# Three reorderings in a fused four-layer plus two-layer forward pass on one Trainium2 core: output pieces, one eviction and two high-part copies moved

## The chip, the cores and the metric

The kernel runs on one core of a Trainium2 chip. The engines of the core work at the same time, each through its own list of instructions in order: TensorE (PE) multiplies matrices into the PSUM banks, VectorE (DVE) and ScalarE (ACT) work on tiles in SBUF and PSUM, GpSimd (POOL) works on tiles in SBUF, and SyncE (SP) issues the loads. They wait for each other on semaphores. The metric is the device time of one execution in microseconds. Lower is better.

## The reference, cut to what matters

Six layers on a sequence of 256 tokens with 1024 channels: convolution, sparse attention, latent attention (MLA), convolution, pooling, stick-breaking attention. The change touches the two softmax attentions and the pooling layer.

```python
def dsa_mixer(...):      # 16 heads of 64; keys chosen by an indexer
    logits = where(chosen, q @ k.T * scale, -inf)
    o = softmax(logits) @ v
    return (o * silu(z)) @ w_out

def mla_mixer(...):      # 16 heads of 96; q and kv from low-rank latents
    logits = where(chunk_visible, q @ k.T * scale, -inf)
    o = softmax(logits) @ v
    return (o * silu(z)) @ w_out

def pooling_mixer(u, w_in, w_group, scale, w_out):
    xb, z = split(u @ w_in, 2)
    xg = xb.reshape(B, S, 4, 512)
    pooled = [causal_pool_minus_self(xg[:, :, g], w) for g, w in enumerate((2, 4, 8, 16))]
    mixed = einsum('bsgi,gio->bsgo', pooled, w_group)
    return (mixed * scale * silu(z)) @ w_out
```

## The kernel before

**Precision.** Every float32 factor of a large matmul is split into a high part and a low part, and a product is three matmuls: high by high, high by low, low by high (`three`). For weights, ACT makes the high part (`whi`, L483 for halves of a unit and L491 for quarters) and DVE subtracts it from the loaded tile to get the low part (`wlo`, L930 and L951).

**Units.** The weights come as a row of units, each a load into one of two `raw` slots, a split, and a run of matmuls. Units are counted by `unit_done`; the load of a unit waits until the slot's earlier unit has its low part (`lo_ready`). A unit of 512 columns is 96 matmuls; `B0`, `C0`, `P0` are the numbers of the first units of the sparse, the latent and the pooling layer.

**The softmax stages** (`paired_heads` on PE, `softmax_heads` on ACT and DVE) run over the 16 heads in steps j = 0 to 9, two heads a step. In step j PE issues the scores of heads 2j and 2j+1, the product with the values for the pair j-2, filler 2j, the transposes of the probabilities of heads 2j-2 and 2j-1 (L2133), and filler 2j+1. DVE does in step j: two minima (L1268, L1272; PE waits for them as `logits`), the gate `ytmp` of pair j-2 (L1253), weight quarters (L951) and two divisions (L1277, L1279). ACT does the exponentials (L705, L707), the copies of the transposes (L720) and the high parts of the weight quarters (L491). POOL splits the gated output into `yh` and `yl` (L1693, L1583).

**Fillers** are matmuls that depend on little and are placed between the dependent ones. First come the pieces of the units for v and z, in parts of 24 matmuls. The last z unit (B0+9, C0+7, called z1) sits in banks 2 and 3 of `acc` and is evicted by `take` (L1038). Then come the output pieces: `attention_out(u, y0, k, half)` is 12 matmuls (k row of the first output unit, half of the columns). Those of half 0 write the `acc` banks that z1 occupied, so the first of them waits for `z_raw`, the semaphore of that eviction. Those of half 1 write the `aux` banks of the scores, so they wait for all 16 `logits`. `out_filler` (L2044) says at which filler number each piece stands: for half 0 the four numbers `at`, for half 1 fillers 15 and 16. The other two pieces of half 1 and the whole second unit follow the loop (`attention_last_out`).

**The pooling stage** runs the list of units x0, z0, x1, mix0, z1, x2, mix1, z2, x3, mix2, z3, mix3, where x and z are columns of the input projection for a group and mix is the group's own matrix. PE starts unit i once unit i-2 has been evicted. For a group, DVE evicts x into `pad` (L1464), POOL forms the pooled sum in several passes (L1747), scales it (L1752) and subtracts (L1753), ACT writes the high part `ph` (L842, `pooled_high`), and POOL the low part `pl` (L1755). The mix unit waits for `pl_ready`. While it handles unit i, ACT also splits the weights of unit i+2. DVE in a z unit takes the low part of unit i+2, then the low part of the earlier y (L1454), then evicts z (L1473).

Of the kernel before, what the change touches and what calls it, by code (L numbers as in the profile page):

```python
# [46 lines left out]
A0, B0, C0, A1, P0, S0, END = 0, 10, 22, 32, 42, 58, 74  # L47
# [51 lines left out]
def build(nc, a, out):  # L99

    ctx = ExitStack()
    with ctx:
# [217 lines left out]
        def quarters(u, halves):  # L320

            return {step: tuple((u, 2 * half + n) for n in range(2)) for half, step in enumerate(halves)}

        SPARSE_SPLITS = {**quarters(B0 + 9, (0, 1)), **quarters(B0 + 10, (2, 3)), **quarters(B0 + 11, (5, 8))}
        MLA_SPLITS = {0: ((C0 + 7, 2), (C0 + 7, 3)), **quarters(C0 + 8, (2, 3)), **quarters(C0 + 9, (5, 8))}
        SPARSE_TANH = {0: (24,), 1: (26,), 4: (28,), 5: (30,)}
        MLA_TANH = {1: (40,), 2: (42,), 4: (44,), 5: (46,)}
        FILLERS = (("v", 1), ("z", 1), ("z", 2), ("v", 2), ("z", 3), ("v", 3))
# [119 lines left out]
        def _(act):  # L448
# [348 lines left out]
            for c in range(4):  # L797
# [3 lines left out]
                h, g = 4 * (c % 2), c // 2  # L801
# [38 lines left out]
            def pooled_high(g):  # L840
                act.wait_ge(sem("pooled"), g + 1)
                A(ph[:, :, :], pad[2][:, :, 16:16 + T], ACT.Copy).then_inc(sem("ph_ready"), 1)  # L842

            for i, (kind, g) in enumerate(POOL_UNITS):
                if kind == "x":
                    split(P0 + i + 2)
                elif kind == "z":
                    split(P0 + i + 2)
                    if g == 0:
                        pooled_high(0)  # L850
                    act.wait_ge(sem("z_raw"), 4 + g + 1)
                    A(arena[:, 39:43, :], arena[:, 39:43, :], ACT.Silu).then_inc(sem("z_ready"), 1)
                else:
                    y_count[0] += 1
                    dst = (yh if g < 2 else y2h)[:, 4 * (g % 2):4 * (g % 2) + 4, :]
                    split(P0 + i + 2, (0, 1) if g == 2 else (0,))
                    if g == 2:
                        pooled_high(3)
                    y_high(y_count[0], dst, arena[:, 39:43, :])
                    if g != 2:  # L860
                        split(P0 + i + 2, (1,))
                    if g < 2:
                        pooled_high(g + 1)
            split(P0 + 14)
            split(P0 + 15)
            split(S0)
# [12 lines left out]
            for i in range(HEADS + 1):  # L879
                if i in FILLED:  # L880
                    kind, n = FILLERS[FILLED.index(i)]
# [18 lines left out]
                if i - 1 in FILLED and FILLERS[FILLED.index(i - 1)][0] == "z":  # L900
                    n = FILLERS[FILLED.index(i - 1)][1]
# [22 lines left out]
        def _(dve):  # L924
# [105 lines left out]
            def take(u, t, name, scale=None, s=None, space=acc):  # L1030

                dve.wait_ge(unit_done, u + 1)
                for c in range(2):
                    src, dst = two(space[:, 2 * (u % 2 if s is None else s) + c, :]), arena[:, t + 2 * c:t + 2 * c + 2, :]
                    if scale is None:
                        ins = TT(dst, src, rb, ALU.mult)
                    else:
                        ins = STT(dst, src, scale, rb, ALU.mult, ALU.mult)  # L1038
                ins.then_inc(sem(name), 1)
# [218 lines left out]
            def softmax_heads(layer, bias, z0):  # L1258
# [23 lines left out]
                for j in range(HEADS // 2 + 2):  # L1282
                    if j < HEADS // 2:
                        minima(2 * j)
                        minima(2 * j + 1)
                    for t in (SPARSE_TANH, MLA_TANH)[layer].get(j - 1, ()):
                        half_silu(t)
                    if j == 9:
                        for u, q in splits[8]:
                            split_quarter(u, q)  # L1290
                    if j >= 2:
                        t = j - 2
                        gate(t, z0, acc[:, 0, T * (t % 2):T * (t % 2) + T], h0 + 2 * t + 2, 4 * layer + t // 2 + 1)
                    for n in range(2):
                        if layer == 0 and j == 4 and n:
                            take(B0 + 9, 28, "z_raw", 0.5)
                        if j - 1 in splits and j < 9:
                            split_quarter(*splits[j - 1][n])
                        if j < HEADS // 2:
                            division(2 * j + n)  # L1300
                    if layer == 1 and j == 0:
                        q_factor(1)
                    if layer == 1 and j == 3:
                        take(C0 + 7, 44, "z_raw", 0.5)

            softmax_heads(0, pick, 24)
            split(C0)
# [62 lines left out]
            for c in range(4):  # L1370
# [16 lines left out]
                if c % 2:  # L1387
                    g = c // 2
# [6 lines left out]
            for c in range(4):  # L1395
# [3 lines left out]
                h, g = 4 * (c % 2), c // 2  # L1399
# [368 lines left out]
        def _(pe):  # L1768
# [274 lines left out]

            def out_filler(f, layer):  # L2044

                u, y0, at = (C0 + 8, 16, (9, 11, 12, 13)) if layer else (B0 + 10, 8, (10, 11, 12, 13))
                if f == at[0]:
                    taken("z_raw", 2 * layer + 2)
                if f in at:
                    attention_out(u, y0, at.index(f), 0)  # L2050
                if 15 <= f < 17:
                    if f == 15:
                        taken("logits", HEADS * layer + HEADS)
                    attention_out(u, y0, f - 15, 1)

            def attention_out(u, y0, k, half):

# [227 lines left out]
            for i in range(HEADS + 2):  # L2285
# [16 lines left out]
                if i < len(FILL):  # L2302
                    f, k0, kn = FILL[i]
# [86 lines left out]
```

## Time and profile before

| | us |
|---|---|
| median of 3 runs | 937.6 |
| lowest and highest | 936.26, 938.47 |
| profiled execution, its own time | 938.38 |
| its span, first to last instruction | 936.7 |
| PE busy, share of the span | 904.1, 97% |
| DVE busy | 648.0, 69% |
| ACT busy | 493.8, 53% |
| POOL busy | 313.6, 33% |
| mean granted TensorE clock | 0.993 of full speed |

PE is busy nearly all the time, so the time can only move where PE waits, or where its clock is granted at half speed. The softmax of the sparse layer lies at about 228 to 287 us of the span, that of the latent layer at about 360 to 415, and the pooling units at 543 to 664. A row of the timeline gives start, duration, engine, line, operation with output and inputs, how many are merged, and in brackets the idle time of the engine before it and what ended it.

### The profile page before, as it was taken

What the parts mean: (1) busy time and instruction counts of PE and PEld (TensorE: products, weight loads), DVE (VectorE), ACT (ScalarE), POOL (GpSimd) and SP (SyncE); (2) the same over time, 40 slices, a digit from 0 to 9 for tenths busy, and PEclk for the clock granted to TensorE, in tenths of its full rate; (3) what the DMA queues carried; (4) which work ended last, traced back from release to release, by engine and by line L of the source; (5) the groups of instructions that cost most, each with busy time, mean ns of one, the idle gap of its engine ahead of it and who ended that gap; (6) DMA issues with size and microseconds to landing.
All of it is one profiled execution on the core that took longest, in us unless ns stands there. A gap on an engine that the chain in (4) does not pass through costs nothing.

```text
span 936.7 us, 16801 instructions
## 1 busy us (share of the span) xinstructions
PE 904.1 (97%) x6761; PEld 850.3 (91%) x6761; DVE 648.0 (69%) x1023; ACT 493.8 (53%) x716; POOL 313.6 (33%) x259
## 2 busy tenths in 40 slices
PE   5999999999989999999999999999999999999996
PEld 5999997788879988779999999999999998989996
DVE  5687666889885789965776676687636645656642
ACT  5544445664765659755444454353535336586632
POOL 7543323373122342233343218775003000223310
PEclk9999999999999999999999999999999999999998
DMA  9796436344314443445695535354663652424411
GB/s 249 194 239 196 180 104 231 124 141 172 143 60 150 141 141 116 133 113 153 163 228 198 180 135 181 135 172 151 247 240 133 236 181 91 172 99 179 156 49 45
DMA packets 123585, 148.70 MB, mean 159 GB/s; under 512 B 9561, under 2 KB 79102, under 8 KB 123518
## 3 DMA queue, kind: packets, MB, share of 16 engines
q1 hardware_dynamic: 121472, 145.63, 48.0%
q10 hardware_dynamic: 1582, 1.12, 0.4%
q0 software_dynamic: 464, 1.02, 0.3%
q8 instruction: 47, 0.77, 0.3%
q14 instruction: 20, 0.16, 0.1%
HBM read 146.70 MB, written 1.05 MB: 158 GB/s over the span
## 4 chain that ended last, share of the span: by engine, by line
PE 62%; DVE 10%; ACT 4%; POOL 3%; issue 1%; ACTq 0%; POOLq 0%; DVEq 0%
PE acc L1770 44%; PE aux L1770 17%; DVE wlo L930 3%; POOL pad L1747 2%; DVE wlo L951 1%; DVE work L1268 1%; DVE work L1279 1%; POOL sqy L1684 1%; ACT work L707 1%; ACT work L705 1%; PE aux L2133 1%; POOL pad L1752 0%; ACT work L720 0%; ACT whi L491 0%; DVE arena L1038 0%
## 5 line engine op out<-in xcount | busy, mean ns | idle before, releaser
L930 DVE TENSOR_TENSOR wlo<-raw,whi 128x2048 fp32r<-128x2048 f32 (+5 forms) x114 | 270.4, 2393 | 90.7 <-ACT whi L483 88.7
L1770 PE MATMUL acc<-xh,whi 128*128 128x256 f32 x1128 | 322.4, 286 | 1.4 <-DVE wlo L930 0.8
L1770 PE MATMUL acc<-xl,whi 128*128 128x256 f32 x1128 | 319.6, 283 | 0.0
L1770 PE MATMUL acc<-xh,wlo 128*128 128x256 f32 x1128 | 319.5, 283 | 0.0
L483 ACT ACTIVATE whi<-raw 128x2048 fp32r<-128x2048 f32 (+5 forms) x115 | 197.8, 1745 | 89.1 <-PE acc L1770 48.3
L1770 PEld LDWEIGHTS acc<-xh,whi 128*128 128x128 f32 x1128 | 216.5, 192 | 3.5 <-issue 1.5
L1770 PEld LDWEIGHTS acc<-xl,whi 128*128 128x128 f32 x1128 | 216.6, 192 | 0.0
L1770 PEld LDWEIGHTS acc<-xh,wlo 128*128 128x128 f32 x1128 | 216.4, 192 | 0.0
L1693 POOL CAST yh<-ytmp 128x256 fp32r<-128x256 f32 x24 | 24.3, 1012 | 207.7 <-DVE ytmp L1532 119.1
L1770 PE MATMUL aux<-yh,whi 128*128 128x256 f32 x288 | 82.6, 287 | 2.0 <-DVE stat L1272 2.0
L1770 PE MATMUL acc<-whi,xh 128*128 128x512 f32 (+1 forms) x208 | 81.4, 391 | 1.6 <-DVE arena L1038 0.5
L1770 PE MATMUL aux<-yh,wlo 128*128 128x256 f32 x288 | 81.9, 284 | 0.0
L1770 PE MATMUL aux<-yl,whi 128*128 128x256 f32 x288 | 81.8, 284 | 0.0
L1770 PE MATMUL acc<-whi,xl 128*128 128x512 f32 (+1 forms) x208 | 78.8, 379 | 0.0
L1770 PE MATMUL acc<-wlo,xh 128*128 128x512 f32 (+1 forms) x208 | 78.8, 379 | 0.0
L951 DVE TENSOR_TENSOR wlo<-raw,whi 128x1024 fp32r<-128x1024 f32 x54 | 66.6, 1236 | 1.7 <-ACT whi L491 1.7
L1770 PEld LDWEIGHTS aux<-yh,whi 128*128 128x128 f32 x288 | 55.6, 193 | 3.3 <-DVE stat L1272 2.5
L1770 PEld LDWEIGHTS aux<-yh,wlo 128*128 128x128 f32 x288 | 55.6, 193 | 0.0
L1770 PEld LDWEIGHTS aux<-yl,whi 128*128 128x128 f32 x288 | 55.6, 193 | 0.0
L491 ACT ACTIVATE whi<-raw 128x1024 fp32r<-128x1024 f32 x52 | 53.2, 1047 | 0.0
L1770 PEld LDWEIGHTS acc<-whi,xh 128*128 128x128 f32 x208 | 39.1, 188 | 12.1 <-issue 4.1
L551 ACT ACTIVATE yh<-arena 128x256 f32 (+1 forms) x16 | 6.7, 418 | 82.2 <-DVE arena L1077 82.2
(344 smaller groups left out, 1726.4 us busy)
## 6 DMA issues: line engine op xcount, KB each, us to landing
raw<-in_a_w_in SPq DMA_DIRECT2D x52, 512.0 KB, 6.6
raw<-in_sb_w_in SPq DMA_DIRECT2D x48, 512.0 KB, 5.2
raw<-in_b_w_in SPq DMA_DIRECT2D x36, 512.0 KB, 5.3
raw<-in_pool_w_in SPq DMA_DIRECT2D x32, 512.0 KB, 5.6
raw<-in_a_w_out SPq DMA_DIRECT2D x16, 512.0 KB, 5.0
raw<-in_pool_w_out SPq DMA_DIRECT2D x16, 512.0 KB, 5.8
raw<-in_sb_w_out SPq DMA_DIRECT2D x16, 512.0 KB, 5.2
raw<-in_b_w_out SPq DMA_DIRECT2D x8, 512.0 KB, 5.0
```

The costliest lines, as they stand in the source:

```text
L483: A(whi[b][:, lo:hi], (raw_third if third else raw[b])[:, lo:hi], ACT.Copy).then_inc(hi_ready, 1)
L491: ins = A(whi[u % 2][:, c * q:c * q + c], raw[u % 2][:, c * q:c * q + c], ACT.Copy)
L705: A(L[:, 0:P], L[:, 0:P], ACT.Exp, bias=st[:, 0:1], scale=nf[:, i:i + 1], accum_out=st[:, 2:3])\
L707: A(L[:, P:W384], L[:, P:W384], ACT.Exp, bias=st[:, 1:2], scale=nf[:, HEADS + i:HEADS + i + 1], accum_out=st[:, 3:4]).then_inc(sem("exp_re ...
L930: TT(wlo[b][:, lo:hi], (raw_third if third else raw[b])[:, lo:hi], whi[b][:, lo:hi].bitcast(F32), ALU.subtract).then_inc(lo_ready, 1)
L951: ins = TT(wlo[u % 2][:, c], raw[u % 2][:, c], whi[u % 2][:, c].bitcast(F32), ALU.subtract)
L1268: ins = V.tensor_tensor_reduce(L[:, lo:hi], S[:, lo:hi], bias[:, lo:hi], -1.0, 3.0e38, ALU.add, ALU.min, st[:, n:n + 1])
L1279: ins = TS(L[:, lo:hi], L[:, lo:hi], st[:, 2 + n:3 + n], None, ALU.mult)
L1684: ins = TT(raw, raw, f.rearrange("p (h d) -> p h d", d=1).broadcast_to([P, 8, 64]), ALU.mult)
L1693: nc.gpsimd.tensor_copy(hi, ytmp[:, :]).then_inc(sem("yh_ready"), 1)
L1747: me.link(TT(pad[dst][:, :, lo:16 + T], pad[src][:, :, lo:16 + T], pad[src][:, :, lo - w:16 + T - w], ALU.add))
L1770: return nc.tensor.matmul(out_, lhsT, rhs, start=start, stop=stop, skip_group_check=True)
```

## The change

1. `MLA_SPLITS`: the second half of the latent layer's first output unit (C0+8) is split in step 4 of ACT and step 5 of DVE, not 3 and 4.
2. Latent softmax on DVE: z1 is evicted (`take`) in step 4 between the two divisions, as in the sparse layer, not at the end of step 3.
3. `out_filler`: the half 0 pieces stand at fillers 11, 12, 13, 15 (sparse, before 10, 11, 12, 13) and 9, 11, 13, 15 (latent, before 9, 11, 12, 13); the first two of half 1 stand at 16 and 17, before 15 and 16.
4. Pooling on ACT: the high parts of the pooled groups 1 and 2 are written in the following z unit, behind the split of the weights of mix1 and mix2, and no longer at the end of the mix unit ahead of it.

```diff
-        MLA_SPLITS = {0: ((C0 + 7, 2), (C0 + 7, 3)), **quarters(C0 + 8, (2, 3)), **quarters(C0 + 9, (5, 8))}
+        MLA_SPLITS = {0: ((C0 + 7, 2), (C0 + 7, 3)), **quarters(C0 + 8, (2, 4)), **quarters(C0 + 9, (5, 8))}
...
-                    if g == 0:
-                        pooled_high(0)
+                    if g < 3:
+                        pooled_high(g)
...
-                    if g < 2:
-                        pooled_high(g + 1)
...
-                        if layer == 0 and j == 4 and n:
-                            take(B0 + 9, 28, "z_raw", 0.5)
+                        if j == 4 and n:
+                            take(C0 + 7 if layer else B0 + 9, 44 if layer else 28, "z_raw", 0.5)
...
-                    if layer == 1 and j == 3:
-                        take(C0 + 7, 44, "z_raw", 0.5)
...
-                u, y0, at = (C0 + 8, 16, (9, 11, 12, 13)) if layer else (B0 + 10, 8, (10, 11, 12, 13))
+                u, y0, at = (C0 + 8, 16, (9, 11, 13, 15)) if layer else (B0 + 10, 8, (11, 12, 13, 15))
...
-                if 15 <= f < 17:
-                    if f == 15:
+                if 16 <= f < 18:
+                    if f == 16:
                         taken("logits", HEADS * layer + HEADS)
-                    attention_out(u, y0, f - 15, 1)
+                    attention_out(u, y0, f - 16, 1)
```

The orders below are the instructions of one engine in a row. The line numbers of the changed kernel are 2 to 4 lower from the pooling code on.

DVE in the latent softmax, around step 4, before (L1038 is the eviction of z1, L1253 the gate of pair 2, L951 a weight quarter, L1277 and L1279 a division):

```order
L1038 SCALAR_TENSOR_TENSOR arena<-acc,r 128x512 x2
L1268 ISA work,stat<-aux,mask 128x128
...
L1253 TENSOR_TENSOR ytmp<-acc,arena 128x256
L951 TENSOR_TENSOR wlo_53<-raw_49,whi_51 128x1024
L1277 RECIPROCAL stat<-stat 128x2
L1279 TENSOR_SCALAR work<-work,stat 128x128
L1279 TENSOR_SCALAR work<-work,stat 128x256
L951 TENSOR_TENSOR wlo_53<-raw_49,whi_51 128x1024
L1277 RECIPROCAL stat<-stat 128x2
```

The same place after:

```order
L1266 ISA work,stat<-aux,mask 128x128
...
L1251 TENSOR_TENSOR ytmp<-acc,arena 128x256
L1275 RECIPROCAL stat<-stat 128x2
L1277 TENSOR_SCALAR work<-work,stat 128x128
L1277 TENSOR_SCALAR work<-work,stat 128x256
L1036 SCALAR_TENSOR_TENSOR arena<-acc,r 128x512 x2
L1275 RECIPROCAL stat<-stat 128x2
```

The eviction went from ahead of the minima of heads 8 and 9 to behind the division of head 8, and the two weight quarters left step 4.

PE in the sparse softmax, steps 5 and 6, before (L2133 transposes of two heads, `yh,whi` the first matmul of an output piece, `work,vB` the product with the values):

```order
L1770 MATMUL acc<-work,vB 64x256 x2
L1770 MATMUL acc<-work,vB 64x128 x2
L1770 MATMUL acc<-yh,whi_51 128x256
...
L1770 MATMUL acc<-yh,wlo_53 128x256
L2133 MATMUL aux<-cst,work 128x128 x6
L1770 MATMUL acc<-yh,whi_51 128x256
```

The same place after:

```order
L1766 MATMUL acc<-work,vB 64x256 x2
L1766 MATMUL acc<-work,vB 64x128 x2
L2129 MATMUL aux<-cst,work 128x128 x6
L1766 MATMUL acc<-yh,whi_51 128x256
...
L1766 MATMUL acc<-yh,wlo_53 128x256
L1766 MATMUL aux<-arena 128x128 x2
```

The output piece that stood ahead of the transposes of heads 8 and 9 is gone from there, and every piece is one place later.

ACT in the pooling stage, from the end of mix0 to x2, before (L842 the high part of a pooled group, the pair `128x1024 x2` the weights of mix1, L852 the silu of z1):

```order
L483 ACTIVATE whi_52<-raw_50 128x2048
L842 ACTIVATE ph<-pad_70 128x1024
L483 ACTIVATE whi_51<-raw_49 128x1024 x2
L852 ACTIVATE arena<-arena 128x1024
L483 ACTIVATE whi_52<-raw_50 128x2048 x2
```

The same place after:

```order
L483 ACTIVATE whi_52<-raw_50 128x2048
L483 ACTIVATE whi_51<-raw_49 128x1024 x2
L842 ACTIVATE ph<-pad_70 128x1024
L852 ACTIVATE arena<-arena 128x1024
L483 ACTIVATE whi_52<-raw_50 128x2048 x2
```

The split of mix1's weights and the high part of group 1 changed places.

## Rows read from the trace of the kernel before

**Rows 1.** The page: the chain that ended last, share of the span by engine.

```profile
PE 62%; DVE 10%; ACT 4%; POOL 3%; issue 1%; ACTq 0%; POOLq 0%; DVEq 0%
```

**Rows 2.** Waits of PE, whole span: waiter, releaser, total us, times, longest.

```profile
PE acc L1770 <- ACT work L720: 3.8, 7, 0.6
...
PE acc L1770 <- DVE arena L1473: 2.0, 1, 2.0
PE aux L1770 <- DVE stat L1272: 2.0, 2, 1.0
```

**Rows 3.** Timeline of PE, pooling: first matmul of mix1 and of z2.

```profile
610.32 0.58 PE L1770 MATMUL acc<-ph,whi 128*128 128x256 f32 x1 [2.04 <-DVE arena L1473]
...
617.62 0.28 PE L1770 MATMUL acc<-xh,whi 128*128 128x256 f32 x1
```

**Rows 4.** Stretches: length, busy of PE, PEld, DVE, ACT, POOL, granted clock, DMA.

```profile
406.00:408.00 2.00, 2.00 (x10) 1.47 (x11) 0.72 (x3) 2.00 (x6) 0.53 (x1) 0.50 0.00 0
...
610.30:612.00 1.70, 1.69 (x8) 1.69 (x9) 1.16 (x2) 1.70 (x2) 0.40 (x1) 0.50 1.13 387
```

**Rows 5.** The chain that ended last: a run of matmuls at full clock.

```profile
664.09 46.08 PE aux L1770 x384
```

**Rows 6.** Timeline of ACT, pooling, around the split of mix1's weights.

```profile
602.04 1.06 ACT L842 ACTIVATE ph<-pad 128x1024 fp32r<-128x1024 f32 x1 [8.73 <-POOL pad L1753]
603.00 1.99 ACT L483 ACTIVATE whi<-raw 128x1024 fp32r<-128x1024 f32 x2
```

**Rows 7.** Timeline of DVE, the same stretch.

```profile
593.35 3.90 DVE L930 TENSOR_TENSOR wlo<-raw,whi 128x2048 fp32r<-128x2048 f32 x1 [0.52 <-ACT whi L483]
604.15 3.66 DVE L930 TENSOR_TENSOR wlo<-raw,whi 128x1024 fp32r<-128x1024 f32 x2 [6.90 <-ACT whi L483]
607.73 1.21 DVE L1454 TENSOR_TENSOR yl<-arena,yh 128x1024 fp32r<-128x1024 f32 x1
608.97 1.29 DVE L1473 TENSOR_TENSOR arena<-acc,r 128x512 f32<-128x512 f32 x2
```

**Rows 8.** Timeline of POOL, the same stretch.

```profile
595.18 4.34 POOL L1752 TENSOR_TENSOR pad<-pad,count 128x1024 f32<-128x1024 f32 x1
599.60 2.41 POOL L1753 TENSOR_TENSOR pad<-pad,pad 128x1024 f32<-128x1024 f32 x1
603.17 2.41 POOL L1755 TENSOR_TENSOR pl<-pad,ph 128x1024 fp32r<-128x1024 f32 x1 [1.17 <-ACT ph L842]
```

**Rows 9.** Timeline of DVE, latent softmax, step 4.

```profile
384.48 1.28 DVE L1038 SCALAR_TENSOR_TENSOR arena<-acc,r 128x512 f32<-128x512 f32 x2
...
387.60 1.22 DVE L951 TENSOR_TENSOR wlo<-raw,whi 128x1024 fp32r<-128x1024 f32 x1
...
388.92 1.10 DVE L1279 TENSOR_SCALAR work<-work,stat 128x128 f32<-128x128 f32 x2
...
391.27 0.55 DVE L1279 TENSOR_SCALAR work<-work,stat 128x128 f32<-128x128 f32 x2
391.73 0.28 DVE L1268 CUSTOM_DVE_ANT_0 work<-aux,mask 128x128 f32<-128x128 f32 x1
```

**Rows 10.** Timeline of PE, latent: transposes 6 and 7, first output piece, scores 10 and 11.

```profile
384.83 0.88 PE L2133 MATMUL aux<-cst,work 128*128 128x128 f32 x6
385.82 0.39 PE L1770 MATMUL acc<-yh,whi 128*128 128x256 f32 x1
...
387.36 1.58 PE L1770 MATMUL aux<-arena 96*128 96x128 f32 x8
```

**Rows 11.** Timeline of PE, sparse softmax, end of the stage.

```profile
277.46 0.39 PE L1770 MATMUL aux<-yh,whi 128*128 128x256 f32 x1 [1.00 <-DVE stat L1272]
...
279.68 0.87 PE L1770 MATMUL acc<-work,vB 128*64 128x256 f32 x8 [0.54 <-ACT work L720]
...
282.01 0.82 PE L2133 MATMUL aux<-cst,work 128*128 128x128 f32 x6
283.46 0.87 PE L1770 MATMUL acc<-work,vB 128*64 128x256 f32 x8 [0.63 <-ACT work L720]
```

## The prediction

> **What bounds the kernel now.** I read the chain that ended last first: PE holds most of it [rows 1], and PE is busy 97% of the span, so a reordering pays only where PE waits or where its clock is granted at half speed. The waits of PE come next [rows 2]. The reader is to see two kinds: one wait of 2.04 us for the eviction of a z unit (L1473), and short ones for the copies of the transposes and the last minima in the two softmax stages. The first sits in the pooling stage: mix1 starts at 610.32 after 2.04 us without work [rows 3]. The granted clock of the stretches around it is the third view. From 610.3 on it stands at 0.50, which is 1.2 GHz of the two levels 1.2 and 2.4, and the same happens at 406 to 408 us, in the tail of the latent softmax [rows 4]. The price of this in pooling: mix1 is 48 matmuls. At full clock a matmul takes 46.08/384 = 0.12 us [rows 5], so mix1 should take 5.76 us, and it takes 617.62 - 610.32 = 7.30 [rows 3]. So the wait cost 2.04 and the lower clock behind it 1.54, together 3.6 us.
>
> Why PE waits there: mix1 reuses the banks of z1, which DVE evicts at 608.97 to 610.26 [rows 7]. DVE was late because it takes the low part of mix1's weights first (604.15 to 607.81), for which ACT gave the high part only at 603.00 [rows 6, 7]. And ACT stood 8.73 us in front of the high part of the pooled group, waiting for POOL, with the split queued behind [rows 6].
>
> **Pooling, the two high parts moved: a gain.** With the split first, ACT waits only for the end of unit z1. Unit x2 (96 matmuls, 11.5 us) ends at 608.28, so z1 ends at 596.8. The split of the two halves takes 1.99 [rows 6], so they are written by 598.8, if the weights have landed by 596.8; their slot was free from the split of x1's unit on, two units before. DVE is free at 597.25 [rows 7]. Its two halves cost about 1.1 each and now fall beside POOL's L1752 and L1753. POOL's L1752 took 4.34 us while DVE's L930 ran to 597.25, L1753 took 2.41 with DVE idle, and both are 1024 columns [rows 7, 8]. So I let them take turns: POOL to 599.5, DVE half to 600.6, POOL's L1753 to 603.1, DVE half to 604.2. The high part `ph` then comes at 603.1 to 604.2. The low part of y (1.2) and `pl` (2.41) [rows 7, 8] take turns again: `pl` is ready at about 607.8, where before it was 605.6. The eviction of z1 (1.29) ends at about 606.8. Unit x2 ends at 608.28, so all is ready by some 0.5 us and the wait of 2.04 goes, and with it what made the clock fall. The gain is 2.04 + 1.54 = 3.6. The split of z2's weights also comes earlier by the same amount and meets POOL's first pass, so I take 3.5. Bounds: 3.6, and 1.5 if 0.5 us of wait are left and the clock falls all the same. Group 2 has no wait of PE before it and `ph` is later by some 2 us with more than 5 to spare, so I cost it at nothing; its cover is unit x3.
>
> The Trainium skill (SBUF — State Buffer, SBUF: two separate sides) says that VectorE with two SBUF inputs and GpSimd take a shared port pair as an exclusive lock for the whole instruction. The 4.34 beside 2.41 agrees. By that rule, if DVE got both its halves in ahead of L1753, `pl` would come at 608.5, 0.2 us too late, and the gain would be 3.4; were there no lock, it would come at about 605.6 and the gain would be 3.6. It leaves the sum where it is.
>
> **Sparse softmax, pieces one place on: a small loss.** Up to the product with the values at 279.68, which waits for ACT's copies [rows 11], the pace is set by DVE and ACT, which the change leaves alone here: the piece no longer in front of the transposes of heads 8 and 9 leaves PE idle, for division 9 is late. From 279.68 on PE's own work counts. Before, it does product, piece, transposes (282.01), waits 0.63, product (283.46), then two pieces. After, one more piece stands behind the transposes: it starts at about 282.6, ends at 284.1, and hides the wait of 0.63. The last product moves from 283.46 to 284.1: 0.7 us lost. The wait of 1.00 for the last minima (277.46) is filled with a piece, but that only brings PE earlier to the same 279.68. Bounds: 0, if PE is held elsewhere anyway, and 2.2 if the idle time up to 279.68 now joins into one stretch of 2 us and the clock falls as it did after 2.04.
>
> **Latent softmax: a loss.** This part has three terms.
> *The eviction behind division 8.* In the kernel before, DVE evicts z1 at 384.48 to 385.76 and PE's first output piece starts at 385.82, right on it [rows 9, 10]. After, DVE starts the minima of heads 8 and 9 at 384.5 (the scores are ready by then, since PE is past them and past the product behind them at 384.83 [rows 10]), then the gate, then division 8. From eviction to the first quarter, two minima and the gate take 387.60 - 385.68 = 1.9, so the gate ends at 386.4. Division 8 costs 0.1 to 0.2 for the reciprocal (388.92 less the end of L951 at 388.82, and its own wait for the exponentials) plus 1.10 while POOL splits the gated pair [rows 9]: 387.8. Then the eviction, 1.28: 389.1. The piece at filler 9 has not moved and needs it, so PE stands from 385.7 to 389.1. Behind it in PE's queue are the scores of heads 10 and 11. The piece is 1.54 (385.82 to 387.36) and the scores 1.5 [rows 10], so they are ready at 392.2. DVE has finished division 9 (0.75) at 389.9 and has nothing else, as the quarters left this step: it idles 2.3 us. From 384.5 to the end of the stage DVE was busy nearly without a gap, and its work up to the last minima is only reordered, the two quarters (1.22 each) coming in step 5. So its idle time goes straight into the end: 2.3, call it 2.4 with worse collisions. Filling PE's later waits gives nothing back, since DVE and ACT set the pace.
> *The clock.* PE has 3.4 us without work there, more than the 2.04 after which the clock fell in pooling [rows 3, 4]. I expect half speed for the piece and perhaps the scores: 12 matmuls cost 12 x 0.12 = 1.4 more at most, less where the fall comes early and is spent idle; I take 1.1. The fall at 406 now costs about 0.8; I let it recur, as the tail keeps waits of the same size.
> *The tail,* as in the sparse stage: one piece more behind transposes 14 and 15, 0.7.
> Sum 4.2; bounds 2.3 (clock kept, and the present fall gone too) and 5.7 (a second fall in the tail, at the 1.54 of pooling).
>
> **Sum.** 0.7 + 4.2 - 3.5 = +1.4 on the profiled execution of 938.38, whose span is 936.7. That execution is 0.8 above the median of 937.6, and I carry the difference over: 939.0. In per cent it is +0.15. What a measurement of this kernel can tell from no change is about 0.2%, 1.9 us.
>
> **Rivals.**
> *Slower, the gain is smaller:* the clock fall in pooling is not in most executions of the kernel before, or comes at another place after. Then pooling gives 2.0 and the sum is 0.7 + 4.2 - 2.0 = +2.9: 940.5. For it: a gap of 1.00 at 276.5 brought no fall [rows 11], so 2.04 may lie near the border. Against it: in this execution the clock was down as soon as work resumed. It decides the sign of the verdict from a pooling gain under 3.0 on. Chance 0.33.
> *Slower, a new fall in a tail:* 1.5 more, 940.5 to 942. For it: waits join, as the piece at 277.46 moves up. Against: the gaps of 1.00 and 0.54 there brought none. Chance 0.07.
> *Faster:* the latent wait is not on the path. If the eviction ended by 386.8, scores 10 and 11 would meet DVE right when it ends division 9, and latent would cost only its tail: 0.7 + 0.7 - 3.5 = -2.1, 935.5. It would take exponentials and division 8 done 2.3 us earlier than the rows allow. With the clock kept in the latent stage and its present fall gone, the sum is 0.7 + 2.3 - 3.5 = -0.5, which is still no change. Chance 0.05.
> *The change does not do what it says:* the orders show that it does; only `pl` too late is left, 0.5 us, inside the range.
>
> **Numbers.** The forecast holds 0.55: no change within 0.2%. Slower holds 0.33 + 0.07 = 0.40, faster 0.05. The low end takes 0.7 + 2.3 - 3.5 = -0.5, down to 937.0; the high end takes the first slower rival with 1 us of a second fall: 941.4.
>
> **What the profile after would show.** Pooling: no wait of PE for the z eviction, mix1 in 5.8 us, clock 1.00 there. Latent: PE waiting some 3.4 us for the eviction (L1036), DVE idle over 2 us before the minima of head 10, clock 0.50 in the next piece. Sparse: PE idle some 1.9 us before the product that stood at 279.68, no wait at the last one. A latent wait under 1 us, or a wait for `pl` in pooling, would prove me wrong.

## The result, and the profile after

The changed kernel takes 938.78 us (median, 936.47 to 940.63), beside 937.61 us of the kernel before on the same chip. The ratio is 1.0014, interval 1.0007 to 1.0020: 1.2 us slower, clear of zero and inside the 0.2% called no change. Forecast were 939.0 and +1.4. The profiled execution has its own time of 939.35 and a span of 937.7 us, 1.0 above the span of before.

The waits of PE over the whole span (waiter, releaser, total us, times, longest). The line numbers of the changed kernel are 4 lower than before on PE and 2 lower in the softmax code of DVE:

```profile
PE acc L1766 <- ACT work L720: 4.0, 5, 1.8
PE aux L2129 <- DVE work L1277: 3.9, 5, 1.2
PE acc L1766 <- DVE arena L1036: 3.4, 2, 2.9
```

Against [rows 2] the wait for the eviction of a z unit in pooling (L1473, 2.0 us) is gone, and one of 2.9 us for the eviction of z1 in the latent softmax (L1036) has come. The copies (L720) are waited for fewer times and once for longer. The waits for the last minima of the two softmax stages (L1272, 2.0 us) are gone too, filled with pieces.

**Pooling.** PE, the first matmul of mix1 and of z2, the rows that answer to [rows 3]:

```profile
612.61 0.28 PE L1766 MATMUL acc<-ph,whi 128*128 128x256 f32 x1
...
618.53 0.36 PE L1766 MATMUL acc<-xh,whi 128*128 128x256 f32 x1
```

No wait stands in brackets, and mix1 takes 618.53 - 612.61 = 5.92 us where it took 7.30. ACT, DVE and POOL in the same stretch, to be read beside [rows 6 to 8]:

```profile
601.35 2.01 ACT L483 ACTIVATE whi<-raw 128x1024 fp32r<-128x1024 f32 x2 [3.53 <-PE acc L1766]
607.40 1.06 ACT L842 ACTIVATE ph<-pad 128x1024 fp32r<-128x1024 f32 x1 [4.04 <-POOL pad L1749]
```

```profile
597.86 3.89 DVE L928 TENSOR_TENSOR wlo<-raw,whi 128x2048 fp32r<-128x2048 f32 x1 [0.54 <-ACT whi L483]
602.51 5.94 DVE L928 TENSOR_TENSOR wlo<-raw,whi 128x1024 fp32r<-128x1024 f32 x2 [0.77 <-ACT whi L483]
608.38 1.21 DVE L1450 TENSOR_TENSOR yl<-arena,yh 128x1024 fp32r<-128x1024 f32 x1
609.62 1.29 DVE L1469 TENSOR_TENSOR arena<-acc,r 128x512 f32<-128x512 f32 x2
```

```profile
599.67 4.36 POOL L1748 TENSOR_TENSOR pad<-pad,count 128x1024 f32<-128x1024 f32 x1
604.11 3.26 POOL L1749 TENSOR_TENSOR pad<-pad,pad 128x1024 f32<-128x1024 f32 x1
608.54 3.33 POOL L1751 TENSOR_TENSOR pl<-pad,ph 128x1024 fp32r<-128x1024 f32 x1 [1.18 <-ACT ph L842]
```

The split of mix1's weights is released by PE's z1 and no longer stands behind `ph`. The two low parts on DVE (5.94 us) and POOL's L1749 (3.26 where it took 2.41) stretch each other. Short stretches of DVE's rows of L928 show where the first half ends (length, busy time, instructions in it, clock, DMA):

```profile
605.10:605.15 0.05, 0.05 (x2) 1.00 0.94 369
605.15:605.20 0.05, 0.05 (x1) 1.00 1.05 410
```

Two instructions overlap up to 605.15 and one is left behind it, so the first half ends there. The eviction ends at 610.91 and `pl` at 611.87; unit x2 ends at 612.61, so what PE needs is there 0.74 us early. The stage is 4.5 us later than in the trace of before when it starts (its first matmul of `xh` by `whi` at 559.03, at 554.53 before) and 0.99 later when it ends (the run of 384 matmuls at 665.08, at 664.09 before): -3.5.

**Latent softmax.** DVE, step 4 and the start of step 5, beside [rows 9]; then PE, beside [rows 10]:

```profile
388.62 0.55 DVE L1277 TENSOR_SCALAR work<-work,stat 128x128 f32<-128x128 f32 x2
389.08 1.28 DVE L1036 SCALAR_TENSOR_TENSOR arena<-acc,r 128x512 f32<-128x512 f32 x2
...
390.48 0.55 DVE L1277 TENSOR_SCALAR work<-work,stat 128x128 f32<-128x128 f32 x2
394.57 0.29 DVE L1266 CUSTOM_DVE_ANT_0 work<-aux,mask 128x128 f32<-128x128 f32 x1 [3.55 <-PE aux L1766]
```

```profile
386.69 0.88 PE L2129 MATMUL aux<-cst,work 128*128 128x128 f32 x6
390.42 0.50 PE L1766 MATMUL acc<-yh,whi 128*128 128x256 f32 x1 [2.85 <-DVE arena L1036]
...
393.07 1.90 PE L1766 MATMUL aux<-arena 96*128 96x128 f32 x8
```

PE stands 2.85 us for the eviction. The piece then takes 393.07 - 390.42 = 2.65 us, where it took 1.54. The scores behind it take 1.90 for 1.58, and DVE idles 3.55 us for them. The granted clock of these stretches, with one later and one in pooling (columns as in [rows 4]):

```profile
390.00:393.00 3.00, 2.58 (x12) 2.58 (x13) 0.99 (x4) 2.61 (x4) 0.00 (x0) 0.59 0.00 0
393.00:396.00 3.00, 3.00 (x21) 2.31 (x20) 1.39 (x9) 0.55 (x3) 0.00 (x0) 0.84 0.03 5
...
408.00:411.00 3.00, 3.00 (x14) 3.00 (x15) 2.52 (x15) 2.31 (x9) 1.03 (x2) 0.50 0.56 138
...
612.00:615.00 3.00, 3.00 (x27) 3.00 (x26) 1.47 (x3) 2.14 (x3) 0.76 (x1) 1.00 0.99 363
```

The fall in pooling is gone, one at 390 has come, and the one in the tail of the latent softmax is there as before, some 2 us later.

**Sparse softmax.** PE at the end of the stage, beside [rows 11] (two products with the values, and between them the transposes of heads 14 and 15):

```profile
280.81 0.87 PE L1766 MATMUL acc<-work,vB 128*64 128x256 f32 x8 [1.79 <-ACT work L720]
283.15 0.82 PE L2129 MATMUL aux<-cst,work 128*128 128x128 f32 x6
285.33 0.87 PE L1766 MATMUL acc<-work,vB 128*64 128x256 f32 x8
```

The idle time is joined into one wait of 1.79 us, and the last product has none. It comes 1.87 us later than the one of 283.46, of which 1.14 is an offset that the trace has before the stage.

In the two traces the parts are therefore: sparse +0.73, latent +2.65 (below), pooling -3.5, and the offset of 1.1 that lies ahead of all three.

### The profile page after: what moved, and what is told of

It reads as the page before. It is cut to its first block, busy times and chain, and to the rows that moved or that the text cites. A ratio compares the mean times of both kernels' runs of the same rounds, so it can differ in the third digit from the quotient of the medians.

```text
span 937.7 us, 16801 instructions
## 1 busy us (share of the span) xinstructions
PE 904.1 (96%) x6761; PEld 851.5 (91%) x6761; DVE 653.5 (70%) x1023; ACT 494.1 (53%) x716; POOL 314.6 (34%) x259
## 4 chain that ended last, share of the span: by engine, by line
PE 64%; DVE 10%; ACT 3%; POOL 1%; issue 1%; ACTq 0%; POOLq 0%; DVEq 0%
PE acc L1766 46%; PE aux L1766 17%; DVE wlo L928 2%; DVE wlo L949 1%; DVE work L1277 1%; DVE work L1266 1%; POOL sqy L1680 1%; ACT work L707 1%; ACT work L705 1%; PE aux L2129 0%; ACT whi L491 0%; DVE arena L1036 0%; DVE sqy L1126 0%; DVE hf L1136 0%; ACT arena L745 0%
## 5 line engine op out<-in xcount | busy, mean ns | idle before, releaser
L928 DVE TENSOR_TENSOR wlo<-raw,whi 128x2048 fp32r<-128x2048 f32 (+5 forms) x114 | 273.6, 2421 | 81.9 <-ACT whi L483 80.0
```

Of the source, the lines that this page charges most:

```text
L928: TT(wlo[b][:, lo:hi], (raw_third if third else raw[b])[:, lo:hi], whi[b][:, lo:hi].bitcast(F32), ALU.subtract).then_inc(lo_ready, 1)
```

## The experiments

**The three parts alone.** Each kernel below is the kernel before with one part of the change.

`pool_only`, the pooling part:

```diff
-                    if g == 0:
-                        pooled_high(0)
+                    if g < 3:
+                        pooled_high(g)
...
-                    if g < 2:
-                        pooled_high(g + 1)
```

> Only the pooling part: the high parts of pooled groups 1 and 2 behind the split of the mix weights; both softmaxes as in the kernel before. Theory A (the wait of 2.04 us and the fall of the clock behind it both go): 3.5 us faster, about 934.1. Theory B (the fall of the clock is not there in most executions of the kernel before): only 2.0 us faster, about 935.6. In the profile both expect no wait of PE for the z eviction.

Measured: 934.51 us beside 937.41, ratio 0.9965 (0.9952 to 0.9978), -2.9 us (-3.3 by the ratio). Span 932.8.

`sparse_only`, the sparse output pieces:

```diff
-(B0 + 10, 8, (10, 11, 12, 13))
+(B0 + 10, 8, (11, 12, 13, 15))
...
-                if 15 <= f < 17:
+                late = 15 if layer else 16
+                if late <= f < late + 2:
```

> Only the output pieces of the sparse softmax one place on (11, 12, 13, 15 and 16, 17). Theory A (one more piece of 1.5 us behind the last copies, hiding a wait of 0.63): 0.7 us slower, about 938.3, first matmul after the last product 0.7 us later against the scores of heads 8 and 9. Rival (the joined idle time lets the clock fall): 1.5 to 2.2 us slower, with granted clock 0.50 behind the idle 1.8 us.

Measured: 937.28 us beside 937.41, ratio 1.0000 (0.9991 to 1.0008). In its trace the same stretch of the stage, from the scores at 256.60 to the last product at 284.61, is 28.01 us, 0.73 more than before and the same as in the whole change. Its times lie in two groups, six at 936.0 to 936.7 with a mean clock of 0.997 or 0.998, and six at 937.9 to 939.2 with 0.995 or 0.996. The 0.7 us is in the rows; in the time it is not shown.

`latent_only`, the split of the weights, the eviction and the pieces of the latent softmax:

```diff
-**quarters(C0 + 8, (2, 3))
+**quarters(C0 + 8, (2, 4))
...
-                        if layer == 0 and j == 4 and n:
+                        if j == 4 and n:
...
-(C0 + 8, 16, (9, 11, 12, 13))
+(C0 + 8, 16, (9, 11, 13, 15))
...
+                late = 16 if layer else 15
```

> Only the latent softmax part: eviction of z1 in step 4, second half of the first output unit split one step later, pieces at 9, 11, 13, 15 and 16, 17. Theory A: PE waits 2.9 us for the eviction and works at half clock behind it; 3.5 to 4.2 us slower in the median, about 941.4. Theory B (the pooling gain was 2.0, so the latent loss is what is left of the sum of 1.2): 2.5 us slower, about 940.1.

Measured: 941.59 us beside 937.41, ratio 1.0047 (1.0034 to 1.0059), +4.2 us. The parts add up: -2.9 + 0 + 4.2 = +1.3, and the whole is +1.2. The forecast was -3.5 + 0.7 + 4.2.

**Which row of the pooling part gives the gain.** `pool_g1` moves only the high part of group 1; that of group 2 stays where it was.

```diff
-                    if g == 0:
-                        pooled_high(0)
+                    if g < 2:
+                        pooled_high(g)
...
-                    if g < 2:
+                    if g == 1:
                         pooled_high(g + 1)
```

> The pooling part for group 1 alone; the high part of group 2 stays at the end of mix1. Theory A (only mix1 was waited for): the whole gain of the pooling part, 3.0 us, about 934.5. Rival (group 2 brings part of it): 935.5 or more.

Measured: 933.60 us beside 937.18, ratio 0.9964 (0.9950 to 0.9978). The gain is there with group 1 alone, and group 2 is worth nothing that shows, as its move was costed.

**Wait or clock in pooling.** `pool_warm` is the kernel before with 14 extra matmuls into a free bank ahead of mix1. The wait is there, filled with work.

```diff
+                if i == 6:
+                    for _ in range(14):
+                        mm(aux[:, 3, 0:T], xh[:, 0, 0:P], xh[:, 0, :], True)
```

> The kernel before with 14 extra matmuls (1.7 us, into a PSUM bank that nobody reads) on PE ahead of the wait for the z1 eviction in pooling; nothing else changes and the wait still ends at the same moment. Theory A (the lower clock behind the wait is a cost of its own, 1.5 us): mix1 takes 5.8 us at clock 1.00 and the kernel is 1.0 to 1.5 us faster, about 936.2, with the wait shrunk to some 0.4. Rival (the fall of the clock is not there in most executions): no change, 937.4.

PE ahead of mix1, and a stretch behind it:

```profile
608.29 1.84 PE L1770 MATMUL aux<-xh 128*128 128x256 f32 x14
610.49 0.39 PE L1770 MATMUL acc<-ph,whi 128*128 128x256 f32 x1 [0.36 <-DVE arena L1473]
```

```profile
612.00:614.00 2.00, 2.00 (x19) 2.00 (x18) 0.64 (x1) 2.00 (x2) 1.92 (x2) 1.00 1.01 376
```

Measured: 936.71 us beside 937.18, ratio 0.9996 (0.9987 to 1.0005). The clock stays at 1.00 behind mix1's start, and mix1 still starts where it did, so the wait of 2.04 is the part that the extra matmuls can't give back. The span falls by 1.2 us, and the median by 0.5 with an interval that holds zero. In the trace mix1 takes 616.34 - 610.49 = 5.85 us, 1.45 less than the 7.30 of before. So the fall costs about 1.5 us in an execution that has it, and the median, with an interval of -1.2 to +0.5 us, has less of it.

How often does the fall stand there? Seven traces are of kernels with the pooling part as before, and each has the wait, 2.04 to 2.08 us. In six of them (before, `sparse_only`, `latent_only`, `evict_only`, `latent_no_evict`, `lat_pieces`) mix1 takes 7.30 to 7.35 us. In `lat_quarters`, behind a wait of 2.06, it takes 5.86 at full clock.

**What of the latent part costs.** `evict_only` moves only the eviction of z1 behind division 8; the quarters and the pieces stay.

```diff
-                        if layer == 0 and j == 4 and n:
-                            take(B0 + 9, 28, "z_raw", 0.5)
+                        if j == 4 and n:
+                            take(C0 + 7 if layer else B0 + 9, 44 if layer else 28, "z_raw", 0.5)
...
-                    if layer == 1 and j == 3:
-                        take(C0 + 7, 44, "z_raw", 0.5)
```

> The kernel before with one edit: the latent z1 evicted in step 4 between the divisions; pieces and weight quarters as before. Theory A (PE stands at the first piece until the eviction, and the scores of heads 10 and 11 behind it come too late for DVE): the eviction now also has a weight quarter ahead of it and ends at about 390.3, but DVE has another quarter to do meanwhile, so it idles 1 to 2 us before the minima of head 10; 1.0 to 2.5 us slower, about 939.2. Rival (the eviction's place costs nothing and the moved pieces or quarters make the latent loss): no change, 937.4.

Its waits between 377 and 416 us:

```profile
DVE work L1268 <- PE aux L1768: 4.5, 3, 2.9
PE acc L1768 <- DVE arena L1038: 4.4, 1, 4.4
```

Measured: 940.48 us beside 937.18, ratio 1.0033 (1.0021 to 1.0044), +3.3. With both quarters still in step 4, PE waits 4.4 us instead of 2.9, and DVE's longest wait for the scores is 2.9.

`latent_no_evict` is `latent_only` with the eviction left at the end of step 3.

> The latent part without its eviction: quarters one step later and pieces at 9, 11, 13, 15 and 16, 17, z1 evicted at the end of step 3 as before. Theory A: the loss of 4.2 us that the latent part alone showed is gone; what is left is its tail, 0.7 us in the rows and nothing in the median, as the sparse part alone: 937.4 to 938.1. Rival (the quarters in step 5 lengthen DVE's path): still 2 us or more slower, over 939.4.

Measured: 939.26 us beside 937.18, ratio 1.0025 (1.0015 to 1.0036), +2.1. There is no long wait for the eviction, and still it is slower. Two kernels take it apart. `lat_quarters` has the first line of the diff of `latent_only` alone:

> The kernel before with one line of the latent part alone: the second half of C0+8 is split in step 4 of ACT and step 5 of DVE. The eviction of z1 and all output pieces stand where they stood. Run to take apart the 2.1 us (939.26 against 937.18) that the latent part without the moved eviction cost. Theory: the ACT splits stand ahead of the tanh that DVE's L1245 waits for (0.9 us there, 0.5 before), and the DVE splits ahead of two later divisions, so most of it is here: 938.2 to 939.2. Rival: it is the pieces, and this kernel is within 0.4 us of the one before.

`lat_pieces` has its pieces alone:

> The kernel before with the places of the latent output pieces alone: half 0 at fillers 9, 11, 13, 15, half 1 from filler 16. The weight quarters and the eviction of z1 stand where they stood. If the two parts add up to the 2.1 us measured for both together, this one gives what the other leaves: by the theory (the quarters cost it) 937.2 to 938.0; by the rival (one more piece of 12 matmuls stands behind the loop's last transposes, and DVE waits for the scores behind a piece) 938.5 to 939.5.

Measured: `lat_quarters` 937.64 us beside 937.41, ratio 1.0008 (1.0000 to 1.0017); `lat_pieces` 938.59 us, ratio 1.0016 (1.0007 to 1.0026). The theory that the quarters cost most of it falls: it is +0.2 for them and +1.2 for the pieces. Together that is 1.4 of the 2.1 by the medians, and 0.0024 of 0.0025 by the ratios. The rows of the table below say +0.57 for the quarters and +0.74 for the pieces, and +1.31, their sum, for both.

**The eviction's wait taken out of the whole change.** `at11` is the changed kernel with one number different, so that the first piece stands one step behind the eviction:

```diff
-(C0 + 8, 16, (9, 11, 13, 15))
+(C0 + 8, 16, (11, 12, 13, 15))
```

> The whole change, but with the latent output pieces at fillers 11, 12, 13, 15, so that the first one no longer stands between the eviction and the scores of heads 10 and 11. Theory A (the loss of the latent stage is the scores held up behind the piece that waits for z1): DVE has no idle time before the minima of head 10, the latent stage costs only its tail of 0.7, and the kernel is 0.7 + 0.7 - 3.5 = 2.1 us faster than before, about 935.5. Rival (the eviction itself, or the two weight quarters moved to step 5, is the cost): no better than the whole change, about 938.8.

Measured: 935.90 us beside 937.41, ratio 0.9990 (0.9981 to 0.9999), 2.9 below the changed kernel (2.2 by the ratios). Its trace has no stretch under full clock until PE's work is over.

`mended` is `at11` with the sparse pieces where they stood in the kernel before.

> The changed kernel with the sparse output pieces back where they stood and the latent pieces of half 0 at fillers 11, 12, 13, 15, so that PE does not come to them before the eviction of z1 is done. The pooling part is in full. Measured so far against the kernel before: the pooling part alone -2.9 us, the whole change with these latent pieces -1.3 us (935.9). Theory: the remaining 1.6 us between the two are the sparse pieces (0.7 us later in the rows) and the latent pieces at the end of the loop, and the moved eviction itself costs nothing: 934.5 to 935.2. Rival: the moved eviction and its divisions behind it cost about 1.5 us even with the first piece out of the way: 935.7 to 936.5. If it comes out under 934.0, the later eviction is a gain once the piece no longer waits for it.

DVE in steps 4 and 5 (the row of L1266 has no bracket), and PE's scores of heads 10 and 11:

```profile
387.01 1.28 DVE L1036 SCALAR_TENSOR_TENSOR arena<-acc,r 128x512 f32<-128x512 f32 x2
...
388.39 0.55 DVE L1277 TENSOR_SCALAR work<-work,stat 128x128 f32<-128x128 f32 x2
388.86 0.28 DVE L1266 CUSTOM_DVE_ANT_0 work<-aux,mask 128x128 f32<-128x128 f32 x1
```

```profile
385.95 1.58 PE L1766 MATMUL aux<-arena 96*128 96x128 f32 x8 [0.46 <-DVE stat L1270]
388.18 0.87 PE L1766 MATMUL acc<-work,vC 128*64 128x256 f32 x8 [0.64 <-ACT work L720]
```

Measured: 934.34 us beside 937.62, ratio 0.9971 (0.9959 to 0.9982). The eviction stands as late as in the changed kernel, but the scores of heads 10 and 11 end at 387.5, before the eviction does, and DVE goes from division 9 straight into the minima. The late eviction costs nothing once no piece in front of the scores waits for it. It is level with `pool_only` (934.51), so it gains nothing either. Between `at11` and `mended` lie 1.6 us for the sparse pieces, where `sparse_only` showed none (-0.8 to +0.8) and the rows 0.7. The 0.7 fits both; 1.6 lies outside the interval of `sparse_only`.

**Wait or clock in the latent softmax.** `lat_warm` is the changed kernel with 22 extra matmuls ahead of the piece at filler 9:

```diff
+                    if layer:
+                        for _ in range(22):
+                            mm(acc[:, 1, 0:T], xh[:, 0, 0:P], xh[:, 0, :], True)
```

> The whole change, with 22 extra matmuls of 128x256 from the tile `xh` into bank 1 of `acc` (the bank is written anew by the next product with the values) just ahead of the first output piece of the latent layer, where PE stood 2.9 us for the eviction of z1. They add work and change no wait of any other engine. Theory, by the rows of the changed kernel (the wait of 2.85 us, then 12 matmuls in 2.65 us where they took 1.54 us before): the half-speed stretch is the cost of the wait beyond its length, so with PE busy the piece takes about 1.5 us, and the kernel is about 1.1 us faster than the changed one, near 937.7. Rival: half-speed stretches vary from execution to execution, and one taken away in the rows is worth little in the median, as with the pooling wait (1.5 us in the row, 0.5 us in the median): 938.2 to 938.8. A second rival: the extra matmuls run on past the eviction, or the stretch falls elsewhere: 939 or more.

PE and DVE at that place:

```profile
385.52 2.88 PE L1766 MATMUL acc<-xh 128*128 128x256 f32 x22
388.63 0.38 PE L1766 MATMUL acc<-yh,whi 128*128 128x256 f32 x1 [0.23 <-DVE arena L1036]
...
390.17 1.48 PE L1766 MATMUL aux<-arena 96*128 96x128 f32 x8
```

```profile
391.25 0.29 DVE L1266 CUSTOM_DVE_ANT_0 work<-aux,mask 128x128 f32<-128x128 f32 x1 [2.02 <-PE aux L1766]
```

Measured: 936.67 us beside 937.41, ratio 0.9997 (0.9989 to 1.0006), where the changed kernel has 1.0014 (1.0007 to 1.0020): 1.6 us less by the ratios, whose intervals do not meet. The piece takes 390.17 - 388.63 = 1.54 us, and DVE idles 2.02 instead of 3.55. So here extra work, which computes nothing that is used, makes the changed kernel faster, and the theory's 1.1 us was, if anything, too small.

**The latent stage in ten traces.** The start is PE's scores of heads 6 and 7, the end PE's product for the last pair of heads. Between them stands the start of the minima of heads 14 and 15 on DVE (the last minima), which parts the stage in two:

| kernel | start | last minima | last product | us | up to the minima | behind them | clock under 1.00 at |
|---|---|---|---|---|---|---|---|
| `pool_g1` (latent as before) | 376.43 | 402.76 | 410.45 | 34.02 | 26.33 | 7.69 | none |
| before | 376.78 | 403.11 | 411.72 | 34.94 | 26.33 | 8.61 | 405 to 411 |
| `lat_quarters` | 376.47 | 403.37 | 411.91 | 35.44 | 26.90 | 8.54 | 402 to 411 |
| `lat_pieces` | 377.31 | 403.64 | 412.07 | 34.76 | 26.33 | 8.43 | none |
| `latent_no_evict` | 377.44 | 404.35 | 412.77 | 35.33 | 26.91 | 8.42 | 402 to 408 |
| `evict_only` | 377.32 | 406.71 | 414.39 | 37.07 | 29.39 | 7.68 | 387 to 396 |
| `latent_only` | 376.89 | 405.94 | 414.35 | 37.46 | 29.05 | 8.41 | 387 to 393 |
| after | 378.64 | 407.82 | 416.23 | 37.59 | 29.18 | 8.41 | 390 to 396, 405 to 411 |
| `lat_warm` | 376.84 | 404.50 | 412.92 | 36.08 | 27.66 | 8.42 | none |
| `mended` | 376.56 | 402.27 | 410.70 | 34.14 | 25.71 | 8.43 | none |

The rows repeat well: `pool_only` and `sparse_only`, with the latent stage as before and no fall in it, take 34.03, `pool_warm` with the fall 34.94, and `at11` takes the 34.14 of `mended`.

Read from the first row: the fall in the kernel before costs 0.92; the changed order with the clock kept costs 36.08 - 34.02 = 2.06; the clock behind the wait costs 37.59 - 36.08 = 1.51 (1.38 in `latent_only`); and the order without the wait costs 0.12. The two columns say what the 0.12 is made of: 0.62 won up to the last minima and 0.74 lost behind them. Behind the minima every kernel with the late pieces takes 8.41 to 8.43, with a fall there or without, and those with the early pieces take 7.68 or 7.69 without a fall.

## Why the prediction was right, step by step

**Pooling, -3.5: right.** The trace shows -3.5, the part alone -2.9 (interval -4.5 to -2.1). The wait and the fall went, group 2 cost nothing. The forecast had `pl` 0.5 us ahead of need, and it was 0.74. The Trainium skill (SBUF — State Buffer, SBUF: two separate sides) gives an exclusive lock for a whole instruction. The trace agrees, and it shows the turns that I forecast. DVE's earlier low part ends at 601.75; POOL's L1748 ends 2.3 later, at 604.03; DVE's first half 1.1 later, at 605.15; POOL's L1749 2.2 later, at 607.37; DVE's second half 1.1 later, at 608.45. These are close to the 2.41 and the 1.1 that I took for each. In the time of the kernel before, 4.5 us earlier, `pl` is ready at 607.4 and the eviction ends at 606.4, where I had 607.8 and 606.8.

**Sparse, +0.7: right in the rows** (+0.73 in both traces), with the wait of 1.79 for the 1.9 forecast and none at the last product. In the time of the part alone it is 0, inside the bounds.

**Latent, +4.2: the mechanism right, three terms off, and the median agrees partly by luck.** PE waits 2.85 us for L1036 where I had 3.4. The failed term there is the division: "1.10 while POOL splits the gated pair" was 0.55, although POOL splits the pair right beside it:

```profile
388.42 0.40 POOL L1689 CAST yh<-ytmp 128x256 fp32r<-128x256 f32 x1 [3.93 <-DVE ytmp L1251]
388.89 0.86 POOL L1579 TENSOR_TENSOR yl<-ytmp,yh 128x256 fp32r<-128x256 f32 x1
```

Here it is POOL's second pass that is the longer one, 0.86 for the 0.73 of before, and the first takes 0.40 for 1.32. In `evict_only`, where a weight quarter still stands between the gate and the division, the division takes 1.10 again (at 388.29) and POOL's first pass 1.32. So the 1.10 went with the quarter ahead of it, which the change takes out of this step.

The trace has +2.65 for the stage, not 4.2. Term by term, from the table:

- *The idle time*, 2.4, is 27.66 - 26.33 = 1.33 with the clock kept, although DVE idles 2.02. The step that failed is that DVE's work up to the last minima "is only reordered", so that its idle time "goes straight into the end". In `mended`, with the same order on DVE and no idle time there, the last minima come 0.62 sooner than before. Which instructions give the 0.62 is not taken apart. -1.1.
- *The clock behind the wait*, taken as 1.1, is 29.18 - 27.66 = 1.52, since the scores and not only the piece run under full clock. +0.4.
- *The tail*, 0.7, is 8.42 - 7.69 = 0.73: right.
- *The fall at 406*, which "I let recur". It recurs, but in the trace after it lies ahead of a product that waits for ACT's copies anyway (0.42 us of wait are left at that product, of the 1.79 in `lat_warm`). The stage behind the minima is 8.41 with it and 8.42 without, so the 0.92 that it cost before is hidden. -0.9.

The median of `latent_only` is nevertheless +4.2. Its traced span is only 2.7 above that of before. What is left comes from which executions were profiled: that of before is 1.0 above the median of its runs in this comparison (938.38 to 937.41), that of `latent_only` 0.5 below its own (941.11 to 941.59). Together these are the 4.2. Part of the 1.0 is the two falls of that execution: against a latent stage at full clock (34.02) the stage of `latent_only` is 3.4 longer.

**The sum.** +1.4 was worked out on one execution. The traces give +0.73 + 2.65 - 3.5 = -0.1, plus an offset of 1.1 ahead of the first part, which the change doesn't touch (a row of the sparse scores stands at 257.32, at 256.18 before; 0.5 of it is in PE's first waits for loads). By the medians of the parts, pooling was 0.6 less of a gain and sparse 0.7 less of a loss than forecast, and latent came out as forecast: the two errors cancel. So the range was earned by the mechanism, and the agreement to 0.2 us (939.0 and 938.78) is luck. The 0.8 us that I carried over from execution to median was right in kind: that execution had both falls, and most have fewer (below). In the forecast's range, -0.5 makes the low end 937.1 and not 937.0, and +2.9 with 1 us more the high end 941.5 and not 941.4.

**The rivals.** The one with a smaller gain in pooling (2.0) is refuted by `pool_only` with -2.9 and `pool_g1` with -3.6, though 2.0 lies only just outside their intervals. On its reason, that the fall is not in most executions, the evidence is divided: six of the seven traces with that wait have the fall, and `pool_warm` finds less than its price in the median. A new fall in a sparse tail stands in the traces of `pool_only` and `latent_no_evict` (276 to 282 us), where that part is as before, and in none of the four traces with the joined wait of 1.79 (after, `sparse_only`, `at11`, `lat_warm`); it belongs to no part of the change. The faster rival, 935.5 for a latent wait off the path, is what `at11` made true by its piece: 935.9.

**What stays open.** The changed kernel's times spread from 936.5 to 940.6, with four below 937, when before has 936.2 to 938.7. Much of this goes with the falls. Traces without a fall during PE's work have a mean granted clock of 0.997 or 0.998, those with one fall 0.995 or 0.996, those with two 0.993 or 0.994, those with more 0.992. The seven executions of the changed kernel at 0.992 or 0.994 take 939.35 to 940.63, the 13 at 0.996 take 936.47 to 939.11. Of 82 executions of before in the experiments, 6 are at 0.997, 55 at 0.995 or 0.996 and 21 at 0.994, where the profiled one has 0.993. The spread within 0.996, and which fall an execution has, the means don't tell. What the sparse pieces cost in the median is open too.

## What to carry to other kernels

Move an eviction later only together with the first instruction, on the engine that fills the gaps, that writes the freed banks: what stands behind that instruction (here the scores) is what the price is paid in. Ask of a half-speed stretch whether it lies ahead of a wait that would be there anyway, and read its price as that of one execution. When the parts of a change have opposite signs, time each alone: here -2.9 and +4.2 lay under a result of no change, and the kernel with the pooling part alone is the better one (934.5 us, and 933.6 with group 1 alone). Cut a stage in two at a row that all traces have, before calling a term absent: here a gain of 0.62 hid a loss of 0.74.

## What the runs showed of the hardware

I had not expected the low clock to move about so much. With the latent stage unchanged it is at 405 to 411 us in the traces of before and of `pool_warm`, and no stretch is under 1.00 in that of `pool_g1` until PE's work is over. The PE row ahead of it in before and in `pool_g1`:

```profile
404.80 0.38 PE L1770 MATMUL aux<-yh,whi 128*128 128x256 f32 x1 [1.00 <-DVE stat L1272]
```

```profile
404.44 0.39 PE L1770 MATMUL aux<-yh,whi 128*128 128x256 f32 x1 [1.00 <-DVE stat L1272]
```

The same wait of 1.00 us has a fall behind it in one and none in the other. Over all the traces, this wait in the latent tail had a fall at its end in three (before, `pool_warm`, `lat_quarters`) and none in three (`pool_g1`, `pool_only`, `sparse_only`). The waits of 1.78 or 1.79 us in the two tails, nine of them, had none at all, and the wait of 2.04 to 2.08 in pooling had one in six of seven. So in these traces the length of a wait of 1 to 2 us does not tell whether the clock falls. Where PE's gap was 2.85 to 4.4 us long (`after`, `latent_only`, `evict_only`), the clock fell late in the gap or at its end in each of the three traces, to the 1.2 GHz level, and with the gap filled it did not (`lat_warm`).

VectorE and GpSimd took turns, instruction by instruction, when both had work on SBUF tiles with two inputs each: GpSimd to 604.03, VectorE to 605.15, GpSimd to 607.37, VectorE to 608.45.
